# Pooling bias in a DeltaNet and pooling backbone step: one rounded product of 64 rows in place of fp32 products of one row

## What is computed

```python
def pool_mixer(h, w_grp, b_grp, scale, rows):
    ...
    pooled = jnp.stack(parts, axis=-2).reshape(B, L, N_POOL_GROUPS, GC).astype(h.dtype)
    y = jnp.einsum('blgc,gce->blge', pooled, w_grp).reshape(B, L, D) + b_grp
    return y * scale

x = layer_norm(ALPHA * x + g1 * y, p['ln_g'][i, 0], p['ln_b'][i, 0])
```

## Time and profile before

| what | value |
|---|---|
| median of 3 executions | 2086.44 us |
| the profiled execution's own time | 2075.06 us |
| its span | 2073.2 us |
| mean granted TensorE clock of the core | 0.971 |
| TensorE (PE) busy | 1908.4 us, 92% |
| VectorE (DVE) busy | 1124.6 us, 54% |
| ScalarE (ACT) busy | 751.4 us, 36% |
| GpSimd (POOL) busy | 411.1 us, 20% |

### The profile page before, as it was taken

One profiled execution on the slowest core, in us unless ns is written; L12 is line 12 of the kernel. 1 busy time (PEld: TensorE's weight loads), 2 busy tenths in 40 slices (PEclk: granted clock), 3 DMA queues, 4 the chain that ended last, 5 costly groups with the idle time before them and its releaser, 6 DMA issues. The chain is left out here.

```text
span 2073.2 us, 39355 instructions
## 1 busy us (share of the span) xinstructions
PE 1908.4 (92%) x14555; PEld 1548.7 (75%) x14556; DVE 1124.6 (54%) x1761; ACT 751.4 (36%) x1287; POOL 411.1 (20%) x316
## 2 busy tenths in 40 slices
PE   6899999999999999999999988999999998899990
PEld 3888888888875488887888766777776777677780
DVE  3566777677674734232222276854457557454338
ACT  2523442443331122221322112744456447443332
POOL 0254334434431222121121334000000000000004
PEclk7899999999999999999999999999999999999995
DMA  8143234233326342353223506966569569654354
GB/s 297 31 147 104 83 116 136 90 98 126 118 81 208 109 142 79 92 151 107 89 92 104 181 13 238 319 213 194 175 210 316 191 200 331 214 176 164 101 173 167
DMA packets 186860, 320.06 MB, mean 154 GB/s; under 512 B 26137, under 2 KB 77729, under 8 KB 186619
## 3 DMA queue, kind: packets, MB, share of 16 engines
q1 hardware_dynamic: 170683, 286.00, 42.0%
q10 hardware_dynamic: 12192, 17.00, 2.4%
q0 software_dynamic: 3744, 13.63, 1.8%
HBM read 283.89 MB, written 32.67 MB: 153 GB/s over the span
## 5 line engine op out<-in xcount | busy, mean ns | idle before, releaser
L1964 ACT ACTIVATE whi<-wring 128x1024 fp32r<-128x1024 f32 (+1 forms) x324 | 314.8, 979 | 407.6 <-PE pp L1270 353.9
L1268 PE MATMUL pp<-whi,xTh 128*128 128x512 f32 (+1 forms) x1152 | 443.8, 385 | 20.0 <-issue 11.1
L1270 PE MATMUL pp<-wlo,xTh 128*128 128x512 f32 (+1 forms) x1152 | 430.7, 374 | 0.0
L1269 PE MATMUL pp<-whi,xTl 128*128 128x512 f32 (+1 forms) x1152 | 430.6, 374 | 0.0
L2627 DVE TENSOR_TENSOR wlo<-wring,whi 128x1024 fp32r<-128x1024 f32 (+1 forms) x180 | 209.5, 1164 | 267.5 <-ACT whi L1964 217.9
L1268 PEld LDWEIGHTS pp<-whi,xTh 128*128 128x128 f32 x1152 | 217.9, 189 | 69.5 <-issue 26.2
L1270 PEld LDWEIGHTS pp<-wlo,xTh 128*128 128x128 f32 x1152 | 218.0, 189 | 38.8
L1269 PEld LDWEIGHTS pp<-whi,xTl 128*128 128x128 f32 x1152 | 218.4, 190 | 34.4
L1268 PE MATMUL pp<-whi,hTh 128*128 128x512 f32 x528 | 212.6, 403 | 7.6 <-DVE hTl L2649 2.4
L1270 PE MATMUL pp<-wlo,hTh 128*128 128x512 f32 x528 | 207.1, 392 | 0.0
L1269 PE MATMUL pp<-whi,hTl 128*128 128x512 f32 x528 | 206.6, 391 | 0.0
(11 more groups left out here) (322 smaller groups left out, 3071.6 us busy)
## 6 DMA issues: line engine op xcount, KB each, us to landing
wring<-in_moe_w_gu SPq DMA_DIRECT2D x320, 256.0 KB, 3.7
wring<-in_ada_w SPq DMA_DIRECT2D x80, 512.0 KB, 4.8
wring<-in_moe_w_down SPq DMA_DIRECT2D x160, 256.0 KB, 3.6
wring<-in_ffn_w_gu SPq DMA_DIRECT2D x80, 256.0 KB, 3.0
wring<-in_dn_w_in SPq DMA_DIRECT2D x128, 128.0 KB, 2.6
wring<-in_ffn_w_down SPq DMA_DIRECT2D x40, 256.0 KB, 3.0
expert_in<-zeros SPq DMA_DIRECT2D x36, 256.0 KB, 3.3
wring<-in_ada_w SPq DMA_DIRECT2D x32, 256.0 KB, 5.3
```

The source lines that it names most:

```text
L1268: pe.matmul(out, hi[:, c0 + c, tt], wh, start=(first and c == 0), stop=False)
L1269: pe.matmul(out, lo[:, c0 + c, tt], wh, start=False, stop=False)
L1270: mm = pe.matmul(out, hi[:, c0 + c, tt], wl, start=False, stop=(last and c == nk - 1))
L1964: act.activation(whi[:, hs, 0:nk, 0:w], wring[:, ring_v.slot(k), 2 * s:2 * s + nk, 0:w], ACT.Copy)\
```

## The change

The bias row of each conditioning is prepared once. GpSimd clears two buffers of 128x512 (left and right half of the columns), which lie over small buffers of earlier stages. ScalarE, behind its last instruction of `ffn(0)`, rounds the matrix of ones into `strict_mask`, waits for the cleared buffers and the bias rows, and writes the rounded bias to row 0 (context) and row 64 (latent) of each buffer. GpSimd waits for that and writes the rest, bias less rounded bias, to rows 32 and 96; it waits for its own writes before it goes on to `root`. TensorE then adds, for each tile, two fp32r products with a contraction of 64 rows: ones times the half of the buffer that belongs to the conditioning. The wait of TensorE on `mask_ready` is dropped; the wait behind it, on `gate_act`, remains. The second bias row is loaded to partition 64 of `hbuf`. Bias buffers, not shown here, are placed by offsets.

```diff
-        pool_bias = (rows[0:1, 7, :], hbuf.rearrange("p t n -> p (t n)")[0:1, 0:D])
+        pool_bias = (rows[0:1, 7, :], hbuf.rearrange("p t n -> p (t n)")[64:65, 0:D])
...
             def decay(h, i):
                 if h == 0 and i == 0:
-                    pe.wait_ge(S["mask_ready"], 2)
                     pe.wait_ge(S["gate_act"], 6)
...
                 out = PP[2 + t % 2]
                 if t == 0:
-                    pe.wait_ge(S["pool_bias_in"], 32)
+                    pe.wait_ge(S["pool_const"], 6)
                     pe.wait_ge(S["pw_scaled"], 2)
                 if t >= 2:
                     pe.wait_ge(S["x2_step"], 2 * (t - 1))
-                for a in range(2):
-                    pe.matmul(out[:, 512 * a:512 * a + 512], cm[0:1, ONES, :], pool_bias[1 if t else 0][:, 512 * a:512 * a + 512],
-                              start=True, stop=False)
+                p = halves(1 if t else 0)
+                for a, pair in enumerate((bias_left, bias_right)):
+                    pe.matmul(out[:, 512 * a:512 * a + 512], strict_mask[p, 0, :], pair[p, :], start=True, stop=False)
...
                 ins.then_inc(S["pw_scaled"], 1)
 
+            for pair in (bias_left, bias_right):
+                ins = pool.memset(pair[:, :].bitcast(F32), 0.0)
+            ins.then_inc(S["pool_const"], 1)
+            pool.wait_ge(S["bias_high"], 1)
+            for k in range(2):
+                for a, pair in enumerate((bias_left, bias_right)):
+                    ins = pool.tensor_tensor(pair[64 * k + 32:64 * k + 33, :], pool_bias[k][:, 512 * a:512 * a + 512],
+                                             pair[64 * k:64 * k + 1, :].bitcast(F32), ALU.subtract)
+            ins.then_inc(S["pool_const"], 1)
+            pool.wait_ge(S["pool_const"], 6)
+
             def root(t, stats, done):
...
             for i, m in enumerate((LT, GT)):
-                act.activation(strict_mask[:, i, :], cmat(m), ACT.Copy).then_inc(S["mask_ready"], 1)
+                act.activation(strict_mask[:, i, :], cmat(m), ACT.Copy)
...
             ffn(0)
+            act.activation(strict_mask[:, 0, :], cmat(ONES), ACT.Copy)
+            act.wait_ge(S["pool_const"], 5)
+            act.wait_ge(S["pool_bias_in"], 32)
+            for k in range(2):
+                for a, pair in enumerate((bias_left, bias_right)):
+                    ins = act.activation(pair[64 * k:64 * k + 1, :], pool_bias[k][:, 512 * a:512 * a + 512], ACT.Copy)
+            ins.then_inc(S["bias_high"], 1)
             for t in range(T):
                 act.wait_ge(S["poolT_ps"], t + 1)
```

More of the change, by code:

```diff
@@ L167, in backbone @@
         ctx.close()
+        ctx = ExitStack()
+        sb("below_bias_left", [P, POOL * P + N_CONST * P - POOL * P + T * D + RING * 4 * 512 + 2 * 2 * KD])
+        bias_left = sb("bias_left", [P, 512], F32R)
+        sb("below_bias_right", [P, 480])
+        bias_right = sb("bias_right", [P, 512], F32R)
+        ctx.close()
         ctx = ctx_all
@@ L381, in backbone @@
             gram_ps gram_sb gm_ready decay_ps ex_ready a_step w_step inv_init inv_swapped off_ready vt_ps vt_sb
-            upd_x_ps upd_y_ps inv_upd kdec_ready mask_ready rhs_ready solve_ps s_read_ps s_add_ps vn_ready o_upd z_side
+            upd_x_ps upd_y_ps inv_upd kdec_ready rhs_ready bias_high solve_ps s_read_ps s_add_ps vn_ready o_upd z_side
             s_upd sp_ready state_in state_out sqo_done sso_done rno_step og_step ogT_ps oT_ready res_ps res_step
```

## The result

The kernel after takes 2089.35 us (median of 16 executions, 2083.78 to 2097.37), the kernel before beside it 2086.11 (16 executions, 2081.13 to 2088.87). The ratio is 1.0021 with a 95% interval of 1.0011 to 1.0030: slower by some 4 us, outside the range of the prediction and on its wrong side. (A ratio is not the quotient of the two medians beside it, which is 1.0016 here; the intervals belong to the ratios.) Every piece of the forecast gain is nevertheless in the profile. A wait that the prediction had priced at nothing is there too.

What follows compares the result with a forecast made beforehand. TensorE, busy 92% of the span, was taken to bound the kernel. A gain of 5.54 us less 1.3 for one clock fall gave 4.2, so 2086.44 became 2082.2 us; range 2079.9 to 2085.6.

Steps and rivals of the forecast that it cites:

- The price of the bias: On TensorE in the pooling stage, each tile's bias would take 0.55 us instead of 1.91, giving up 1.36 us.
- What of it reaches VectorE: At VectorE's waits for the linear map over tiles 0 to 4, 5.54 of TensorE's 6.8 us would arrive.
- The clock: TensorE's opened gap around the router would bring one fall to half clock, costing 0.8 to 1.7 us, 1.3 in the middle.
- What is added: Preparation on GpSimd and ScalarE would end near 1198.7, before the first root at 1201.86, and cost nothing.
- The price of the subtractions: GpSimd's four subtractions would take 1.30 us each, 5.2 in all, ahead of the first root.
- the cover: Slack on GpSimd before VectorE would wait: 3.2 us ahead of the first root plus 4.75 behind it, some 8 in all.
- its only slower rival: TensorE's clock might stay at half from 1242 to the pick products, 1.69 us per fall, 2100 at worst; chance 0.05.

Runs made afterwards that it cites:

- the products alone: Kernel after without ScalarE's five and GpSimd's four preparing instructions, so the bias is left out of the result: 2078.90 us against 2079.54 before, ratio 1.0003.
- the gap filled: Kernel after with ScalarE's preparation moved earlier and six unread fp32 products behind the router's first product: ratio 0.9982 to the kernel before, 0.9977 when run again.
- the last group: Kernel before, kernel after, and the early preparation without and with work in the router's gap, run on one chip: ratios 0.9998, 1.0022, 0.9979, 0.9977.
- the second group: Four kernels on one chip beside the kernel before (2085.44 us), among them the kernel after again: 2087.89 us, ratio 1.0012.
- the roots first: Kernel after with GpSimd's four subtractions moved behind the roots of tiles 0 to 2, ScalarE's copies still late: 2088.37 us against 2085.44 before, ratio 1.0013.
- the preparation alone: Kernel after with the old one-row fp32 products on TensorE, ScalarE and GpSimd still preparing the rounded bias: 2087.72 us against 2079.54 before, ratio 1.0041.

## Why the prediction was wrong, point by point

**The price of the bias** was right: 0.55 forecast, 0.65 measured, against 1.91 before.

**What of it reaches VectorE** was right: 5.54 forecast, 5.33 in six profiles that have no other trouble in the stage. The waits behind tile 0 are zero in all of them. At tile 0, 1.2 us remain there, 1.1 by the forecast. A part of this was luck: 1.7 us of the 5.54 are a fall of the clock under full work that the prediction had seen in one execution only, and it turned out to be in every profile with the old products.

**The clock** was right in kind and at the upper end in size. The forecast took one fall in the router, 0.8 to 1.7 us, 1.3 in the middle; it was 1.6 in seven of the eight profiles that have the gap of 3.61 us, and none in the eighth, that of the products alone. With the gap filled it was in neither of two. The Trainium skill's page "TensorE: Matmul & The Clock Gate" (section on why this matters) has the rule that gaps between bursts of matmuls cost the clock. The seven profiles agree (66.08 with the gap, 64.46 with work in it), the eighth doesn't (64.46 with the gap), so the gap makes the fall likely here and not certain. Another fall, at tile 1's pooling product behind the held root, wasn't forecast at all.

**What is added** is the step that failed: "I cost all of it at nothing", and the root held in GpSimd's queue cost VectorE 4.9 us. It said that "ScalarE has nothing to do between `ffn(0)` and the first pooled tile" and let the copies run at 1190. The free stretch had been read from the timeline, where ScalarE's last instruction ended at 1178.9 and the next began at 1212.75. These are the rows of the kernel before:

```profile
1178.30 0.63 ACT L1964 ACTIVATE whi<-wring 128x512 fp32r<-128x512 f32 x1 [5.74 <-PE pp L1270]
1212.75 1.02 ACT L2117 ACTIVATE pT<-pp 128x1024 f32<-128x1024 f32 x1 [33.82 <-PE pp L1385]
```

Only instructions show there, and the 33.82 us are put down to what ended them. In the code ScalarE passes `high_after` four more times in that stretch, for the last halves of the down projection. Each call waits for its products before it finds that there is no slot left to round. Such a wait without an instruction leaves no row. It ends with the last product of `ffn(0)`, at 1200.9 in the profile after, right when GpSimd's roots are due. The Trainium skill's page "Perfetto Trace Analysis" (section on the per-instruction lifecycle) says that semaphore waits lie outside of what the profiler reports for an instruction; the two rows agree.

The price of the subtractions was right (5.2 us forecast, 5.4 from 1203.49 to 1208.92), and so was the list of who is queued behind whom. Only the end was 10 us off (1198.7 forecast, 1208.9 measured). A smaller slip made it worse: the cover was counted up to L2766 at 1207.49, but VectorE waits for the root ahead of the first of the two instructions, at 1206.21 (L2764), so that 3.5 us and not 4.75 were left behind it. The prediction wrote down what would follow if the cover were gone, but gave that case neither a price nor a chance; its only slower rival was the clock.

**The sum with the measured terms.** At the third expert hrow: -5.33 for the products, +5.0 for the held root, and +1.6 for the pooling product that the longer idle time put at half clock, makes +1.3; the profiles show +1.26. With the router's fall, +1.62, it is +2.9 at the router's result; +2.88 and +3.0 are measured. The whole, 1.0021 at first and 1.0022 in the last group, is 4.4 and 4.6 us with intervals that go down to 2.3 and 1.7, so it agrees; 1.0012 in the second group does too.

**Against the base.** Of the 14.6 us between the first two profiles, -1.3 lie ahead of the stage, +2.9 are the stage's, +4.1 the stall, and +8.9 lie behind the first expert's first product. Of these, 2.2 go with the stall too: behind it that expert's thirteenth product starts 5.07 us behind the first in the place of 2.84, most of the way at half clock. For the whole part behind the first expert's first product the kernel before took 783.9, 787.7 and 789.9 us in three profiles (the last with the stall) and the kernel after 792.8, 791.1 and 787.2, so a good part of it is spread between executions. Whether the change adds something there isn't separated.

## What to carry to other kernels

Before new work is put into the idle time of an engine, go through its instruction stream for waits that issue nothing: the free stretch of a timeline begins at the last of these waits, not at the last instruction. Where the new work feeds a second engine, look at which of that engine's later instructions is due first, and price the whole block ahead of it from the real start. In this kernel GpSimd's idle time beside a busy VectorE wasn't free either, even for one partition.

## What was not expected of the hardware

GpSimd's subtractions of one partition by 512 columns slowed VectorE, in the kernel with the roots first. The instruction with both inputs in SBUF took 1.68 us in the place of 0.69 (L2606) or 2.17 in the place of 1.28 (L2791). The one that reads an input from PSUM (L2604, 0.68) and the statistics with one input (L2614, 0.69) kept their time. The Trainium skill's page "GPSIMD Engine Reference" (section on specifications) names VectorE instructions with two SBUF inputs among those that contend; the trace agrees, and shows that one partition is enough. Which engine stood followed who had begun: L2789 has two inputs in SBUF as well, but began at 1210.25, ahead of the third subtraction, and took 1.31 us, near its 1.25 elsewhere, while that subtraction took 2.15. No run varied this order on purpose.

The start of the experts has two forms, 10.7 and 14.7 us behind the first pick product, with the same program. In seven of the nine profiles with the longer one ScalarE's second copy starts 3.6 to 4.0 us after TensorE's last pick product, and the profile calls what released it "remote"; in the other two the last pick product itself came late. The longer form costs more than its 4 us: the first expert's thirteenth product starts 4.4 to 5.3 us behind its first, most of the way at half clock, in the place of 2.84. Within each of the three groups all profiles show one form (the products alone, with other routing, can't be compared). Each group had a chip of its own, so chip and loading aren't told apart. What makes the difference wasn't found.

The fall of TensorE's clock under full work, which the prediction took from one execution, was in each of the three profiles of the kernel before, at tile 2, 3 and 1, and at tile 2 in the preparation alone, which has the old products too. It cost the same 1.7 us each time. With the short bias it was in none of ten profiles between tile 0's linear map and the router. Whether the products of one row are what brings it wasn't tested.
